# A decoder trunk on eight cores: who empties the first value tiles, two tiles of filler ahead of a layer's first scores, and another VectorE instruction for part of the attention masks

## The reference

```
h = rms_norm(x, g_pre);  proj = h @ w_in            # q/k/v of 12 dilated and 4 block-sparse heads, 2 gates
o_a = dilated_attention, 3 groups of 4 heads: (window 128, dilation 1), (512, 4), (2048, 16)
      query t sees t, t-d, ..., t-window;  p = exp(q.k/8 - slope*d*steps), masked outside the window
      the three groups are added per head slot, weighted by their softmax denominators
o_b = MoBA: own block of 256 keys (causal) + the top 3 past blocks by q . mean(k)
y = (sigmoid(gate_a) * (o_a @ W_A) + sigmoid(gate_b) * (o_b @ W_B)) @ w_out;  x = x + rms_norm(y)
h = rms_norm(x);  u = gelu(causal_conv3(h @ w_gate)) * (h @ w_up);  x = x + rms_norm(u @ w_down)
```

## Time and profile before

| what | value |
|---|---|
| median of 3 runs | 3797.01 us |
| profiled execution, its own time | 3794.95 us |
| its span (first to last instruction of the slowest core) | 3793.6 us |
| spans of the 8 cores | 3790.2 to 3793.6 us |
| TensorE busy | 3708.5 us, 98% |
| VectorE busy | 2008.8 us, 53% |
| ScalarE busy | 1756.4 us, 46% |
| GpSimd busy | 876.3 us, 23% |
| mean granted TensorE clock | 0.996 to 0.998 |

### The profile page before, as it was taken

How to read it: one execution, slowest core, us unless ns; L and a number is a source line. 1 busy time by engine, 2 the same in 40 slices (tenths; PEclk the granted TensorE clock), 3 DMA queues, 4 the chain that set the end, 5 groups by cost and what they waited for, 6 DMA issues and landing times.

```text
span 3793.6 us, 55772 instructions; the slowest of 8 cores (3790.2 to 3793.6 us)
## 1 busy us (share of the span) xinstructions
PE 3708.5 (98%) x19888; PEld 1806.4 (48%) x19888; DVE 2008.8 (53%) x2985; ACT 1756.4 (46%) x3389; POOL 876.3 (23%) x1484
## 2 busy tenths in 40 slices
PE   5999999999999999999999999999999999999999
PEld 4644444444554444444465444444446544444444
DVE  4354666465346466646434646754643454675463
ACT  2457345254346635535334753543533475354351
POOL 2331332111133133211113223221111322331110
PEclk9999999999999999999999999999999999999999
DMA  6234788454323478864542358874542336796442
GB/s 151 29 77 72 154 172 162 115 99 90 84 35 74 74 164 181 147 170 78 123 95 53 57 93 170 176 133 128 78 106 52 56 59 108 157 193 120 101 69 73
DMA packets 304009, 410.38 MB, mean 108 GB/s; under 512 B 150704, under 2 KB 167344, under 8 KB 303728
## 3 DMA queue, kind: packets, MB, share of 16 engines
q0 software_dynamic: 118656, 190.89, 33.3%
q1 hardware_dynamic: 185088, 215.92, 20.8%
HBM read 500.56 MB, written 67.63 MB: 150 GB/s over the span
## 4 chain that ended last, share of the span: by engine, by line
PE 94%; DVE 3%; ACT 1%; issue 1%; DMA 1%; POOL 0%; SPq 0%; DVEq 0%; POOLq 0%; ACTq 0%
PE psum L396 35%; PE psum L1297 16%; PE psum L1025 12%; PE psum L643 11%; PE psum L551 6%; PE psum L676 5%; PE psum L620 5%; PE psum L965 3%; PE psum L707 1%; DVE s_arena L722 0%; DMA s_xr<-x 0%; ACT s_arena L716 0%; DVE s_arena L388 0%; DVE s_arena L997 0%; DVE s_hb L473 0%
## 5 line engine op out<-in xcount | busy, mean ns | idle before, releaser
L396 PE MATMUL psum<-s_hT,s_slabs 128*128 128x512 bf16 x5632 | 1223.9, 379 | 2.6 <-DVE s_arena L1258 2.6
L396 PEld LDWEIGHTS psum<-s_hT,s_slabs 128*128 128x128 bf16 x5632 | 551.4, 98 | 668.6 <-issue 5.3
L1297 PE MATMUL psum<-s_arena 128*128 128x512 bf16 x2816 | 609.1, 379 | 0.0
L1025 PE MATMUL psum<-s_hT,s_slabs 128*128 128x512 bf16 x2048 | 489.7, 379 | 0.4
L1247 DVE SCALAR_TENSOR_TENSOR s_arena<-s_arena,s_convw 128x512 f32<-128x512 f32 x352 | 264.2, 751 | 425.3 <-ACT s_arena L1239 425.2
L643 PE MATMUL psum<-s_hT,s_slabs 128*128 128x512 bf16 x2048 | 473.1, 379 | 12.0 <-DVE s_km L833 4.6
L1297 PEld LDWEIGHTS psum<-s_arena 128*128 128x128 bf16 x2816 | 275.6, 98 | 332.2
L424 ACT ACTIVATE s_hb<-psum 128x1024 bf16<-128x1024 f32 x128 | 131.0, 1024 | 524.0 <-PE psum L1297 344.5
L433 DVE SCALAR_TENSOR_TENSOR s_tz<-psum,s_stat,s_gpost 128x1024 f32<-128x1024 f32 x128 | 164.0, 1282 | 362.7 <-POOL s_stat L412 362.6
L976 ACT ACTIVATE s_arena<-psum 128x512 bf16<-128x512 f32 (+3 forms) x640 | 306.3, 542 | 86.3 <-PE psum L965 63.2
L676 PE MATMUL psum<-s_arena 128*128 128x128 bf16 (+2 forms) x1840 | 314.7, 264 | 7.6 <-DVE s_arena L997 2.4
(11 more groups left out here) (75 smaller groups left out, 3992.9 us busy)
## 6 DMA issues: line engine op xcount, KB each, us to landing
s_slabs<-w_in_r POOLq DMA_DIRECT2D x224, 256.0 KB, 4.8
xs<-s_xr SPq DMA_DIRECT2D x96, 512.0 KB, 3.3
s_xr<-xs SPq DMA_DIRECT2D x96, 512.0 KB, 5.5
s_slabs<-w_gate_r POOLq DMA_DIRECT2D x176, 256.0 KB, 4.4
s_slabs<-w_up_r POOLq DMA_DIRECT2D x176, 256.0 KB, 5.2
s_xr<-x SPq DMA_DIRECT2D x64, 512.0 KB, 6.3
s_arena<-w_down POOLq DMA_DIRECT2D x88, 256.0 KB, 6.3
y<-s_xr SPq DMA_DIRECT2D x32, 512.0 KB, 2.9
```

The source lines that it names most:

```text
L396: inst = nc.tensor.matmul(out, lhsT=l_, rhs=r_, start=(i == 0), stop=(i == n - 1))
L1025: inst = nc.tensor.matmul(ps[b], lhsT=buf[:, kc * 128:(kc + 1) * 128], rhs=hT[:, kc, tsl], start=(kc == 0), stop=(kc == 7))
L1297: inst = nc.tensor.matmul(ps[zb + n], lhsT=uT[:, kc, i * 128:(i + 1) * 128], rhs=wdn[kc][:, n * 512:(n + 1) * 512], start=(kc == 0), stop= ...
```

## The change

Four things change. `merge` gets a `lead`: an amount of filler that runs before the first step. For the first unit of a pass it is 1.8, which is two value tiles of the next group. `evac_n` is `[3, 4]` during the first value projection of passes 2 to 4, and `[1, 2]` again for the q and k after it. The mask products of g = 1 and 2 are issued as `scalar_tensor_tensor` (P times 1.0 times mask) and those of g = 0 stay `tensor_tensor`; all are written with merged dimensions. For g = 2 the probabilities and the mask lie densely in 512 and 256 elements, where they lay in halves of rows of 256.

```diff
-def merge(main, *fills):
-    live = [[gen, ratio, 0.0] for gen, ratio in fills]
-    for cost in main:
+def merge(main, *fills, lead=0.0):
+    live = [[gen, ratio, lead] for gen, ratio in fills]
+
+    def run():
         for f in list(live):
-            f[2] += cost * f[1]
             while f[2] > 0:
                 try:
                     f[2] -= next(f[0])
                 except StopIteration:
                     live.remove(f)
                     break
+    run()
+    for cost in main:
+        for f in live:
+            f[2] += cost * f[1]
+        run()
...
+        Pd16 = [carve(o * KB, 256, BF16).rearrange("p (k h q) -> p k h q", k=2, h=2) for o in (68, 70, 72, 86)]
...
+            Pu = Pd if g < 2 else Pd16
...
-                    dm = dmask[:, head:head + 2, :].rearrange("p (o h) q -> p o h q", o=1)
                     for (a, b, nq), te in zip(pieces, tE):
                         DVE.wait(te)
-                        tM = DVE.do(nc.vector.tensor_tensor(out=P[:, a:b, :, 0:nq], in0=P[:, a:b, :, 0:nq],
-                                                            in1=dm[:, :, :, 0:nq].to_broadcast([128, b - a, 2, nq]), op=ALU.mult))
+                        if b - a == 2:
+                            w = 2 * nq
+                            c0 = head * 256 if g < 2 else 2048 + 256 * sp
+                            p_ap = P.rearrange("p k h q -> p k (h q)")
+                            m_ap = dmask[:, :, :].rearrange("p (o a) b -> p o (a b)", o=1)[:, :, c0:c0 + w].to_broadcast([128, 2, w])
+                        else:
+                            p_ap = P[:, a, :, 0:nq]
+                            m_ap = dmask[:, head:head + 2, 0:nq]
+                        if g == 0:
+                            tM = DVE.do(nc.vector.tensor_tensor(out=p_ap, in0=p_ap, in1=m_ap, op=ALU.mult))
+                        else:
+                            tM = DVE.do(nc.vector.scalar_tensor_tensor(out=p_ap, in0=p_ap, scalar=1.0, in1=m_ap, op0=ALU.mult, op1=ALU.mult))
...
             if pre is None:
+                evac_n[:] = [3, 4]
                 drain(v_proj(l, 0, ALLB, vt[0], p_wait))
+                evac_n[:] = [1, 2]
...
-                merge(dil_unit(g, sp, QK[i % 2], qt[(g, sp)], vt[g], acc_free, res), (fill, max(total, 20.0 if i == 3 else 0.0) / 6.9))
+                merge(dil_unit(g, sp, QK[i % 2], qt[(g, sp)], vt[g], acc_free, res), (fill, max(total, 20.0 if i == 3 else 0.0) / 6.9), lead=1.8 if i == 0 else 0.0)
...
+    d16 = dmask[:, 8:12, 0:128].copy()
+    dmask[:, 8:12, :] = 0.0
+    dmask[:, 8:10, :] = d16.reshape(128, 2, 256)
```

More of the change, by code:

```diff
@@ L710, in dil_unit @@
                     sl = (p0 + step) % 4
-                    P = Pd[sl]
+                    P = Pu[sl]
                     s4 = psum[:, 0:2048].rearrange("p (k h q) -> p k h q", k=2, h=2)
@@ L741, in dil_unit @@
                             for i, (kt, pc) in enumerate(lst):
-                                P = Pd[(p0 + kt // 2) % 4]
+                                P = Pu[(p0 + kt // 2) % 4]
                                 inst = pv_mm(ps[ub][:, col:col + 128], V, kt, hd, P[:, kt % 2, h, pc:pc + 128],
```

## The result

The changed kernel takes 3819.15 us (median of 4 runs, 3817.22 to 3820.94) and the kernel before 3796.73 (4 runs, 3794.55 to 3797.14): a ratio of 1.006, 95% interval 1.0043 to 1.0078, some 22 us slower. The forecast was 3796.8 with a range of 3788 to 3807. The slowdown lies outside it.

What follows compares the result with a forecast made beforehand. TensorE was taken as the bound, busy 3708.5 of 3793.6 us, with some 15 to 20 us within reach. Terms 0 - 4.0 + 8.2 - 4.4 = -0.2 gave a median of 3796.8 us, range 3788 to 3807.

Steps and rivals of the forecast that it cites:

- First value copies: Before the tenth value tile in passes 2 and 4: waits stay, 0 us; bounds 0 and a gain of 2.6.
- The lead: Start of each pass: two early value tiles cover the first scores' wait and shift later copies, -4.0 us.
- The term for passes 2 and 4: Lead, unit (0,0): step 0's 0.41 wait stays, step 1 starts with VectorE and gets a wait, +0.9 us in both.
- Products of g = 1: Units (1,0) and (1,1): slower scalar-tensor-tensor products lengthen TensorE's waits, +8.2 us; bounds 0 and 11.
- The term of (1,0): Unit (1,0): step 0's wait grows 0.59 us per pass, 2.4 us; one more step per pass costs 2.2.
- Products of g = 2: Unit (2,1): new products escape GpSimd's adds, so both TensorE waits for L833 go, -4.4 us; other end +5.5.
- Not held: g = 2, unit (2,1): GpSimd's adds do not hold the new products, which take 0.75 us; -4.4 us.
- rival 1: Units (2,0) and (2,1): GpSimd's adds hold the new products too, +9.7 us in all, 3806.7 us; chance 0.23.
- sign of idle time in MoBA or the gates: After the units: no TensorE idle time expected there; if any appears, the forecast is wrong.
- rival 2: Mask products: new ones run at the old rate; 3793.0 us if held, 3788.6 if not; chance 0.17.
- rival 3: Unit (0,0): the lead only moves the wait, 3.8 us more than forecast, 3800.6 us; chance 0.10.
- rival 4: First value copies of passes 2 and 4 pay after all, -2.6 us, 3794.2 us; chance 0.08.

Runs made afterwards that it cites:

- e11: Kernel before with only the first value copies changed, three in four on ScalarE; 3796.0 us (a single execution).
- e12: Kernel before with the first three value tiles of passes 2 to 4 copied by ScalarE, three in four after that, nothing else; 3793.7 us, ratio 0.9993.
- e3: e1 plus a one-column exp on ScalarE right after the last q/k copy; 3793.3 us, ratio 0.9984 to the kernel before.
- e6: Kernel before with all products changed and GpSimd's adds of g = 1 and 2 left out, no lead; spans 3790.0 to 3794.4 us on cores 0 to 3.
- e8: e4 with the lead of two value tiles also ahead of unit (1,0); 3794.6 us, ratio 0.9997 to the kernel before.
- e1: Changed kernel with tensor-tensor products everywhere; layout, lead and first copies stay as changed; 3796.4 us, ratio 0.9993 to the kernel before.
- e4: e3 with the first three value tiles of passes 2 to 4 copied by ScalarE; 3790.2 us, ratio 0.9971 to the kernel before.
- e2: Kernel before with only the products and their layout changed; 3817.6 us, ratio 1.0044.
- e5: Kernel before with the new products for g = 1 alone, no lead, first copies as before; 3818.0 us, ratio 1.0058.

## Why the prediction was wrong, step by step

**First value copies: 0. Right.** The second tile is still VectorE's and its wait is 1.31 us in pass 2. e11 has nothing but 0.35 us in pass 4. e12 shows what the bound of the forecast named, a gain of 2.6 if both waits went: with the second tile on ScalarE it is 2.8.

**The lead: -4.0 forecast, -0.5 measured** (-0.7, +0.8, -1.6 and +1.0 by pass). The waits of the scores did go. The term for passes 2 and 4 missed the table load: the working looked at which engine copies first behind the mask, and not at what else stands on ScalarE ahead of exp. Each of the two passes paid 1.33 us for it, as e3 shows, 2.7 of the 3.5 us that are missing. The 0.8 left is missing in passes 1 and 3, where waits of 1.2 and 1.9 us were to go. Most of it is a new wait of 0.3 us in each, of a q/k tile for ScalarE's copy (L649 for L390, 0.6 us in 2 waits on core 7; the list of before has none). The table load was even a row of the forecast, as a delay that goes in pass 3; it was not asked where it is when a filler copy precedes exp.

**Products of g = 1: +8.2 forecast, +17.9 measured without the clock. Here the prediction failed.** The rate was nearly right: 1.23, 0.69 and 0.42 us for 1024, 512 and 256 elements, for 1.28, 0.75 and 0.49 forecast. The term of (1,0) was right, 4.4 for 4.6, its wait at step 0 going from 0.85 to 1.40 us. The part of (1,1) that slower products cost by themselves was right too, 3.1 (e6) for 3.6. The step that failed is the sentence that the value matmuls "come two steps after their mask, 7 us, and don't notice". That is so in the middle of a unit. Its last two steps have no scores left, so TensorE is ready for the last product 1.0 us after its start (1174.55 less the wait of 1.08, from 1172.47), and it now starts behind an add. e6 against the changed kernel gives this its price: 10.3 us.

**Products of g = 2: -4.4 forecast, about +0.5 measured.** They are held: a product of 512 elements takes up to 1.97 us with the adds, and without them (e6) never over 0.69. "Not held" rested on one short row, L1247 within L412, and that row could not carry it: GpSimd read one element per partition in it. Whether that, or the f32 operands, is why L1247 kept its time was not tried. So the mechanism of rival 1, that the new products are held like the old ones, was the true one, with a chance of 0.23. But its place was wrong: in (2,1), where it put most of its +5.5, TensorE's waits for the block sums grow only from 4.6 to 5.7 us over the whole span, and the decisive unit is (1,1), where no product had been held at all and now both pieces of the last one are, in every pass. The Trainium skill ("SBUF — State Buffer", section "Who interferes with whom") has the rule that decided: of a VectorE instruction with two SBUF inputs and a GpSimd one that reads SBUF, whichever starts second is blocked. The runs agree: the product from 1172.47 is held by the add from 1172.33, and the two adds, with the product's first piece between them, take 3.44 us, where the pair in e8 takes 2.99. Over the eight cores of the changed kernel all 306 products that were held began within an add, and of the 320 that began ahead of an add and ran into it none was held. e8 has an exception, told at the end.

**The clock: 0 forecast.** On 7 of 8 cores the new waits at the end of (1,1) are followed, in one to three passes, by a stretch of 3.4 us at half clock, which costs 1.7 us (half of it; 1.5 to 1.9 by the stages). The slowest core has three such places (from 1178.2, 2113.4 and 3058.9 us), and its stages from (2,1) to the gelus are 5.2 us longer for them than those of cores without one; core 7 has none, and is the one with +17.8. The prediction has no term for this, and its sign of idle time in MoBA or the gates does not mean it: the stretches lie at the turn from (1,1) to (2,1), with TensorE busy in them.

**The sum.** 18.3 us of stages, up to 5.2 us of clock and, on the slowest core, 1.0 us of the late load stand against -0.2. The errors are +0.35 for the copies, +3.5 for the lead, +9.7 for g = 1, +4.9 for g = 2, and the clock. The other rivals fell: the same rate as before (rival 2) by the durations; the lead that only moves the wait (rival 3) by pass 3, where it gains 1.6 us, though its price of 3.8 us is near the 3.5 that are missing and in passes 2 and 4 a wait did grow, by the table load; first copies that pay (rival 4) by the wait that stays.

## What to carry to other kernels

A VectorE instruction that is made longer, or later, is to be laid against GpSimd's timeline at every place where it runs, first of all where the slack ends, at the last steps of a unit: who starts 0.1 us sooner decided 2.6 us per pass here. Before filler is put ahead of an activation, look where its table load stands, and pin it with an activation of one column. A gain of filler, and an engine chosen for a copy, hang on the first few items in the queue, so work out the order item by item rather than by shares: the three-in-four on ScalarE did nothing here, and three particular tiles gave 2.8 us.

## What was not expected of the hardware

**Half clock behind short waits.** Core 0 of the changed kernel in pass 4, just behind unit (1,1): window, its length, busy us of PE, PEld, DVE, ACT and POOL, granted clock, DMA share, GB/s:

```profile
3046.00:3056.70 10.70, 8.26 (x66) 4.05 (x64) 9.68 (x11) 5.40 (x11) 6.40 (x6) 1.00 0.21 28
3056.80:3060.20 3.40, 3.40 (x10) 1.22 (x8) 2.10 (x3) 1.43 (x3) 3.39 (x2) 0.50 0.87 171
3060.20:3064.00 3.80, 3.80 (x28) 1.57 (x26) 1.72 (x3) 1.78 (x3) 0.04 (x1) 1.00 0.83 187
```

TensorE was idle for 2.4 us in the first window, most of it in two waits close together, and then the clock granted is 0.50 (1.2 GHz) for 3.4 us and 1.00 (2.4 GHz) again. Before, between the first 75 us and the last 5, only one such place exists, at about 2461 us on 6 of 8 cores, behind a wait of 2.62 us. e1, e3 and e4 have that one alone; in e2 and e5, with the new products, all eight cores have it behind (1,1) in passes 1 and 2 as well; e6, which has no double wait, has none at (1,1). So two waits of 1.1 and 1.3 us can cost 1.7 us more than they show, in some passes and on some cores. What separates them I can't tell.

**A hold of 3.75 us.** In e8 a product is held by two adds, though it began at 156.10 and they at 156.57. So the order of starts, which decides in (1,1), doesn't explain it. In that moment GpSimd was issuing a DMA (155.99, 0.57 us). The issue alone doesn't hold a product: in the kernel before, on its eight cores, 109 products begin within one with no add behind them, and none is held. In e8 all 16 that begin within an issue with an add right behind it are, one in pass 1 and one in pass 3 on each core, and they take some 3.75 us each. Why these wait for both adds stays open.
